# A hybrid block kernel: its compression weights in buffers of their own, and every weight remainder on VectorE

## The reference, cut to what matters

```python
proj = einsum('bsd,de->bse', rmsnorm(x), w_in[l])      # 1024 -> 3476 columns
# four heads of mLSTM, four of block attention, four of "native sparse attention" (NSA)
# NSA: two 64-wide streams kc, vc are compressed, blocks of 32 tokens at stride 16 -> 15 blocks
c = t.reshape(B, S // 16, 16, 64)
blocks = concatenate([c[:, r:15 + r] for r in range(2)], axis=2) + pe_
hid = silu(blocks.reshape(B, 15, 2048) @ w1_)          # w1_: 2048 x 128, one for kc, one for vc
return hid @ w2_
# the queries attend to the 15 compressed blocks (p_c), to selected blocks, to a window
x = x + mix @ w_out[l]
x = x + square(relu(rmsnorm(x) @ w_ff1[l])) @ w_ff2[l]
```

## Time and profile before

| | us |
|---|---|
| median of three runs | 1168.91 |
| lowest and highest of them | 1166.6, 1170.94 |
| the profiled execution, its own time | 1161.15 |
| its span in the trace | 1159.3 |
| granted TensorE clock, mean over the span | 0.984 |

### The profile page before, as it was taken

The page is one execution under the profiler, slowest core; times in us unless marked ns, Lnnn a source line. Parts: engine busy times, 40 slices in busy tenths (PEclk is TensorE's granted clock), DMA queues, the critical chain, the costliest instruction groups (busy, mean ns, idle before and its releaser), DMA issues.

```text
span 1159.3 us, 17421 instructions
## 1 busy us (share of the span) xinstructions
PE 1109.0 (96%) x6816; PEld 967.6 (83%) x6816; DVE 722.1 (62%) x1257; ACT 622.8 (54%) x981; POOL 115.5 (10%) x99
## 2 busy tenths in 40 slices
PE   8899989999999899989999999999999989999997
PEld 6787769899988787769899888798988767989885
DVE  4897667555556887667555656576355566744555
ACT  5545746544545445746444545465657446656562
POOL 0324110000000324110000000004000000040000
PEclk9999999999999998999999999999999989999999
DMA  8635235565666435236556565454443445544531
GB/s 300 192 94 179 86 116 183 184 194 184 182 184 186 142 93 177 87 117 199 181 186 187 178 197 183 157 170 145 128 145 110 145 146 164 154 137 120 154 127 55
DMA packets 88958, 181.15 MB, mean 156 GB/s; under 512 B 8669, under 2 KB 19805, under 8 KB 88877
## 3 DMA queue, kind: packets, MB, share of 16 engines
q1 hardware_dynamic: 87437, 175.78, 49.0%
q10 hardware_dynamic: 1440, 4.26, 1.0%
HBM read 178.97 MB, written 1.05 MB: 155 GB/s over the span
## 4 chain that ended last, share of the span: by engine, by line
PE 75%; DVE 13%; ACT 6%; issue 3%; POOL 1%; DMA 1%; DVEq 0%; POOLq 0%; SPq 0%; ACTq 0%
PE bank L757 22%; PE bank L759 21%; PE bank L758 21%; DVE w_lo L1572 2%; ACT w_hi L1207 2%; PE bank L834 2%; PE bank L872 1%; PE bank L919 1%; DVE vecs L1581 1%; DVE xn L1856 1%; PE bank L1015 1%; PE bank L1146 1%; DMA raw<-in_w_in 1%; PE bank L929 1%; PE bank L928 1%
## 5 line engine op out<-in xcount | busy, mean ns | idle before, releaser
L1572 DVE TENSOR_TENSOR w_lo<-raw,w_hi 128x1024 fp32r<-128x1024 f32 x296 | 365.3, 1238 | 312.3 <-ACT w_hi L1207 308.2
L1207 ACT ACTIVATE w_hi<-raw 128x1024 fp32r<-128x1024 f32 (+1 forms) x320 | 334.6, 1052 | 253.7 <-PE bank L759 222.6
L757 PE MATMUL bank<-h_hi,w_hi 128*128 128x256 f32 x896 | 259.9, 290 | 4.5 <-DVE w_lo L1572 2.1
L758 PE MATMUL bank<-h_lo,w_hi 128*128 128x256 f32 x896 | 255.2, 285 | 0.0
L759 PE MATMUL bank<-h_hi,w_lo 128*128 128x256 f32 x896 | 255.1, 285 | 0.0
L757 PE MATMUL bank<-w_hi,h_hi 128*128 128x512 f32 (+1 forms) x448 | 182.0, 406 | 5.8 <-DVE h_lo L1591 5.3
L757 PEld LDWEIGHTS bank<-h_hi,w_hi 128*128 128x128 f32 x896 | 173.6, 194 | 9.7 <-DVE w_lo L1572 3.1
L759 PE MATMUL bank<-w_hi,h_lo 128*128 128x512 f32 (+1 forms) x448 | 176.4, 394 | 0.0
L758 PE MATMUL bank<-w_lo,h_hi 128*128 128x512 f32 (+1 forms) x448 | 175.9, 393 | 0.0
L758 PEld LDWEIGHTS bank<-h_lo,w_hi 128*128 128x128 f32 x896 | 173.8, 194 | 0.5
L759 PEld LDWEIGHTS bank<-h_hi,w_lo 128*128 128x128 f32 x896 | 173.5, 194 | 0.0
(11 more groups left out here) (283 smaller groups left out, 1401.6 us busy)
## 6 DMA issues: line engine op xcount, KB each, us to landing
raw<-in_w_in SPq DMA_DIRECT2D x144, 512.0 KB, 3.9
raw<-in_w_ff SPq DMA_DIRECT2D x128, 512.0 KB, 4.1
raw<-in_w_out SPq DMA_DIRECT2D x40, 512.0 KB, 3.2
raw<-in_cmp_w SPq DMA_DIRECT2D x8, 512.0 KB, 4.5
raw<-in_w_in SPq DMA_DIRECT2D x8, 404.0 KB, 4.1
x_sb<-in_x SPq DMA_DIRECT2D x2, 512.0 KB, 7.4
gain<-in_norm_ffn ACTq DMA_DIRECT2D x2, 512.0 KB, 6.9
gain<-in_pre_norm ACTq DMA_DIRECT2D x2, 512.0 KB, 4.7
```

Source lines behind the costliest of these rows:

```text
L757: pe.matmul(out_ap, s_hi, m_hi, start=start, stop=False, **kw)
L758: pe.matmul(out_ap, s_hi, m_lo, start=False, stop=False, **kw)
L1207: act.activation(slot(w_hi, u), slot(raw, u), ACT.Copy).then_inc(hi_ready, 1)
L1572: dve.tensor_tensor(slot(w_lo, u), slot(raw, u), slot(w_hi, u).bitcast(F32), ALU.subtract)\
```

## The change

1. **Compression weights.** They leave the ring of `raw`. Four buffers that are idle at that time hold them: the two halves of `xn`, columns 1024 to 1535 of `mix`, and `gain`. SP loads each quarter (512 KB) with two transfers, behind the issue of units 5, 7, 9 and 11 of the layer (`load_cmp_weights`). Ahead of the first it waits until the last transpose of `xn` is done, ahead of the third (layer 0) until `sel` has been copied out of `mix`. The load of the next `gain` is issued by ScalarE after the compression products instead of after the norm.
2. **Compression products.** The blocks are stationary (32 columns), the weights move (128 columns); the sixteen chunks of each stream go in turn to four column groups of the array, at partitions 0, 32, 64 and 96 of one bank. ScalarE copies the four partial sums to `hid_parts`, and two short products with a 0/1 matrix (`C_SUM4`) add and transpose them (`hidden`).
3. **Turn 4** needs no doubled copy: eight products with the even or the odd columns of the identity put even tokens on partitions 0 to 63 and odd tokens on 64 to 127 (`even_odd_tokens`), and VectorE writes `blocksT` with two instructions instead of eight.
4. **Order.** Turn 4 goes from p 13 to p 12, `cmp` from p 16 to 18 to p 14 and 15, `hidden` to p 16, `cmp_kv` to 18, `cmp_kT` to 19, `cmp_s` and `cmp_soft` to 20, `cmp_o` from 25 to 26. The two `cmp_s` steps become one that alternates between them. The first `conv` waits for the compression products.
5. **`cmp_o`** is added straight to `mix` columns 768 to 1023.
6. **Remainders.** All 24 of GpSimd's go to VectorE.

```diff
-                proj_unit(0, l, w_in[l], j, bp, q, COLS1, "pool" if (p % 3 and p >= 13) or p in (9, 11) else "vector")
+                proj_unit(0, l, w_in[l], j, bp, q, COLS1, "vector")
...
-                if p == 11:
-                    step("vec_b", l, "copy")
                 if p == 12:
+                    single(0, "turn", l, 4)
                     single(4, "turn", l, 0)
...
+                if p == 14:
+                    use(("hidden_parts", l), 0)
+                    step("cmp", l, 0)
+                if p == 15:
+                    step("cmp", l, 1)
+                    done(("hidden_parts", l))
+                    step("hidden_parts", l)
                 if p == 16:
-                    use(("hidden", l), 2)
-                    cmp_unit(0, 0)
+                    single(3, "hidden", l)
...
+            def load_cmp_weights(n):
+
+                for l in range(L):
+                    at = n - unit_no["proj", 0, l, PROJ1[0], 0] - CMP_FIRST
+                    if at in (0, 2, 4, 6):
+                        k = at // 2
+                        if k == 0:
+                            filled(sp, ("norm", 2 * l, 1, 1))
+                        elif k == 2 and l == 0:
+                            sp.wait_ge(sel_ready, 1)
+                        w1 = cmp_w1[l, k // 2].rearrange("(h b a p) e -> h p b a e", p=P, a=4, b=2)[k % 2]
+                        for b in range(2):
+                            sp.dma_start(cmp_homes[k][:, b, :].rearrange("p (a e) -> p a e", e=P), w1[:, b]).then_inc(cmp_loaded[k], 16)
...
+            def even_odd_tokens(l, key):
+
+                for i in range(NT):
+                    drained(pe, ("proj", 0, l, 6, i))
+                ps = open_bank(key)
+                for v in range(2):
+                    for i in range(NT):
+                        for odd in range(2):
+                            mm = pe.matmul(ps[HD * odd:HD * odd + HD, v * P + HD * i:v * P + HD * i + HD],
+                                           rest[:, i, 1032 + HD * v:1032 + HD * v + HD], ident[:, odd:P:2], start=True, stop=True,
+                                           skip_group_check=True)
+                close(mm, key)
...
-                        for a in range(8):
-                            mm = pe.matmul(ps[:, 16 * v:16 * v + NC_CMP], w[:, a, :], blocksT[:, v, 8 * half + a, :],
-                                           start=(half == 0 and a == 0), stop=(half == 1 and a == 7))
-                        finish_unit(mm, s)
+                        for a in range(16):
+                            if a % 8 == 0:
+                                pe.wait_ge(cmp_loaded[2 * v + a // 8], 32 * (l + 1))
+                            g, at_col = 32 * (a % 4), NC_CMP * (16 * v + a)
+                            mm = pe.matmul(ps[g:g + 32, v * P:(v + 1) * P], blocks[:, at_col:at_col + 32], cmp_weights(v, a),
+                                           start=a < 4, stop=a >= 12, skip_group_check=True)
...
+                    elif kind == "hidden_parts":
+                        free(act.activation(hid_parts[:, :, :], src(s)[:, 0:T].rearrange("p (v e) -> p v e", v=2), ACT.Copy), s)
+                        load_gain(2 * l + 1)
...
-                        dst = mix[:, :, 1024:1280]
-                        free(dve.tensor_copy(dst, src(s)[:, :].rearrange("p (i c) -> p i c", i=NT)), s)
+                        dst = mix[:, :, 768:1024]
+                        free(dve.tensor_tensor(dst, dst, src(s)[:, :].rearrange("p (i c) -> p i c", i=NT), ALU.add), s)
```

More of the change, by code:

```diff
@@ L71 @@
 C_C01 = C_CNEG + NT * NC_CMP
[L72 removed]
+C_SUM4 = C_C01 + NT * NC_CMP
+C_END = C_SUM4 + 16
 def constants():
@@ L242, in m_values @@
             single(b, "mlstm", l, "O", h)
[L244 to L247, removed]
         for bp, j in enumerate(PROJ1):
@@ L598, in hybrid_blocks @@
         diag_ready = sem("diag_ready")
+        cmp_loaded = [sem(f"cmp_loaded{n}") for n in range(4)]
         half_neg_set = sem("half_neg_set")
@@ L1005, in _ @@
                     elif kind == "cmp":
[L1007 to L1010, removed]
+                        v = s[2]
+                        if v == 0:
+                            ps = open_bank(("hidden_parts", l))
                             pe.wait_ge(blocks_ready, l + 1)
-                        pe.wait_ge(raw_arrived[unit_no[s] % SLOTS], 16 * (unit_no[s] // SLOTS + 1))
-                        w = slot(raw, u)
-                        for a in range(8):
-                            mm = pe.matmul(ps[:, 16 * v:16 * v + NC_CMP], w[:, a, :], blocksT[:, v, 8 * half + a, :],
-                                           start=(half == 0 and a == 0), stop=(half == 1 and a == 7))
-                        finish_unit(mm, s)
+                        for a in range(16):
[4 more added lines that the diff above has]
+                                           start=a < 4, stop=a >= 12, skip_group_check=True)
+                        if v == 1:
+                            close(mm, ("hidden_parts", l))
+                    elif kind == "hidden":
+                        ps = open_bank(s)
+                        drained(pe, ("hidden_parts", l))
+                        for v in range(2):
+                            mm = pe.matmul(ps[:, 16 * v:16 * v + 16], hid_parts[:, v, :], const[:, C_SUM4:C_SUM4 + 16],
+                                           start=True, stop=True)
+                        close(mm, s)
                     elif kind == "cmp_kv":
@@ L1031, in _ @@
                     elif kind == "cmp_s":
-                        if s[2] == 0:
-                            drained(pe, ("turn", l, 5))
-                            drained(pe, ("cmp_kT", l))
-                        ps = open_bank(s)
-                        b = HD * s[2]
+                        if s[2]:
+                            continue
+                        drained(pe, ("turn", l, 5))
+                        drained(pe, ("cmp_kT", l))
+                        ps = [open_bank(("cmp_s", l, odd)) for odd in range(2)]
                         for i in range(NT):
```

98 lines of the change are left out of this document (46 added, 52 removed).

## The result

The changed kernel took 1138.42 us (median of four, 1137.7 to 1139.48), the kernel before, beside it, 1169.74 (1166.6 to 1170.94): ratio 0.9737, interval 0.9715 to 0.9759. Over all 73 executions of the kernel before that stood beside the experiments its median is 1167.9, from 1159.9 to 1173.6, and the mean granted clock falls from 0.987 in the shortest to 0.973 in the longest. The profiled one, 1161.15 us at 0.984, was one of the short ones; the median of the 73 is some 7 us longer.

A forecast was written before the change was run, and what follows sets the result against it. Up to 125 us TensorE's work and VectorE's lateness were taken to set the pace together. TensorE's 11.4 us per layer, capped by VectorE at 7.6, less 1.1, gave 6.5, 13 in all: 1168.91 - 13 = 1155.9 us, range 1147 to 1168.

The forecast's parts named there:

- The median of runs lies 7.8 above the profiled one, and I move it by the same: Last step, whole kernel: median stays 7.8 us above the profiled execution, so 1168.91 - 13 = 1155.9.
- VectorE allows less: Up to 125 us: VectorE's ledger (2.4) and its 5.22 us wait cap the gain at 7.6 us per layer.
- in-order waits: VectorE, being in order, also waits for `w_hi` where GpSimd did: 1.1 us per layer taken off, leaving 6.5.
- TensorE's ledger: TensorE's savings to 125 us: 2.4 + 3.8 + 0.1 + 1.8 + 1.7 + 1.6 = 11.4 us per layer.
- nearly free for VectorE: GpSimd's remainders moved to VectorE: 13.2 us added ahead of the last convolution, 13.0 of holding gone, net +0.2 per layer.
- Products: Compression products on TensorE, 64 instructions at 0.06 us in four column groups: 3.8 us instead of 7.56, -3.8 per layer.
- rival D: Column groups do not overlap: compression products cost 7.9 us instead of 3.8; -9 in all, 1160 us; chance 0.12.
- A: The forecast itself: -13 us, own range -7 to -19 (1150 to 1162); chance 0.48.
- Order of the chain: Compression chain two positions earlier: TensorE's waits shrink by 1.7 us for `kc_n`, 1.8 for `m_rows`, per layer.
- Clock: One of the two half-clock stretches up to 125 us goes: -1.6 us per layer.
- Rival E: Both half-clock stretches of each layer go and VectorE keeps up: 4 us more per layer, -21, 1148; chance 0.09.
- Rival C: VectorE's in-order queue waits at each of the 24 moved remainders: 25 us against 13, +12, 1181; chance 0.13.

The follow-up runs named there:

- e16: e7 with all four groups of 15-column compression products together at p 16 in bank 7: 18.6 us above e14.
- e12: e7 with 16 of the 32 float32 compression products per layer left out: 8.8 us less than e7.
- e8: The kernel before with own buffers for the compression weights, 24 remainders still on GpSimd: 1175.4 us, ratio 1.0076.
- e1: The kernel before with only GpSimd's 24 remainders moved to VectorE: ratio 0.9994.
- e7: The kernel before with own buffers for the compression weights and all remainders on VectorE: ratio 1.0013.
- e6: The changed kernel with the old form of the compression products (15 columns moving, no partial sums, bank 7): ratio 0.9841, 10.6 us above the changed kernel.
- e17: The changed kernel plus 32 unread float32 products per layer with 15 moving columns: 7.4 us from e18, 21.0 us lost to clock.
- e18: The changed kernel plus 32 unread float32 products per layer with 128 moving columns, one column group: 7.4 us from e17, 12.3 us lost to clock.
- e15: e14 with the 24 remainders back on GpSimd: 8.9 us above e14.
- e14: e13 with turn 4 as before: 11.2 us above the changed kernel.
- e10: The changed kernel with the four copies, four transposes and eight instructions of turn 4 as before: 1144.1 us.
- e3: The changed kernel with one column group instead of four and partial sums of 32 rows: ratio 0.977, 2 us above the changed kernel.
- e11: The changed kernel with 16 of the 32 float32 compression products per layer left out: no gain.
- e9: The changed kernel with the compression chain at its old places (products at p 16): 1145.3 us.
- e13: e9 with the partial sums in bank 7: equals e9's 1145.3 us.

## Why the prediction was wrong

The miss of 17.5 us has two parts of equal size.

**The median was moved by the same as the profiled execution (8.8 us).** "The median of runs lies 7.8 above the profiled one, and I move it by the same": this step failed. The profiled execution after took 1139.48 and the median is 1.1 below it. The kernel before has executions over 14 us apart, by their clock; so have e16 (11 us), e12 and e8 (7 each), with the same 15-column products. The kernels in the new form spread over 1 to 5 us. The offset went with the change, but the form of the products alone does not explain it: e1, e7 and e6 have the old form too and spread over 2.5 (ten executions), 4.5 (ten) and 0.7 us (four). That this form keeps the clock down is shown by e17 against e18; how the clock varies from execution to execution was only seen, and its cause stays open.

**The sum of the profiled execution (8.7 us).** 1148 was forecast for it. The mixing stages gave 19.7 us instead of 13, the feed-forward stages 2.5 instead of 0, the start and the rest took 0.6 back. The step that failed is "VectorE allows less": at most 7.6 us per layer, 6.5 with the in-order waits. To the start of `conv_silu`, counted from the squares, layer 0 went from 104.99 to 96.38 us and layer 1 from 105.70 to 93.81: 8.6 and 11.9. The windows of both layers (columns as in the earlier trace rows), before:

```profile
20.06:125.05 104.99, 96.88 (x626) 84.78 (x626) 84.13 (x211) 53.81 (x107) 34.62 (x25) 0.97 0.52 157
367.12:472.82 105.70, 97.96 (x624) 86.21 (x624) 82.01 (x206) 52.59 (x106) 35.00 (x25) 0.95 0.45 137
```

and after:

```profile
21.23:117.61 96.38, 88.46 (x642) 76.88 (x642) 80.64 (x213) 53.92 (x109) 5.76 (x13) 1.00 0.56 168
357.56:451.37 93.81, 87.92 (x632) 77.23 (x631) 79.66 (x207) 53.04 (x107) 5.92 (x13) 0.98 0.51 158
```

VectorE's busy time fell by 3.5 and 2.4 us, near the 2.4 of the ledger. Its idle time, what is left of each window, fell by 5.1 and 9.5, where the prediction allowed 5.22 at most and took 1.1 off. It had read that limit from one wait in layer 0; in layer 1 VectorE was idle for 23.7 us before and 14.2 after. TensorE's ledger said 11.4, close to layer 1, but its waits, of which 2.4 + 1.8 + 1.7 were to go, hardly went: TensorE's idle time in these windows went from 8.1 to 7.9 and from 7.7 to 5.9 us, as new waits (2.05 for `hid_parts`) took the place of old ones. What fell is its busy time, by 8.4 and 10.0: shorter products and time at 1.2 GHz.

Term by term:

- *Remainders, "nearly free for VectorE".* Right as a sum: over the whole trace VectorE's busy time in e1 against before is 723.0 against 722.1 with 24 remainders (24.3 us in their group) more, so 23.4 of holding went from its other work. Wrong as a price: undone in the changed kernel they cost 20.5 us, 15.4 at full clock and 5.1 of clock. A likely reason, argued and not shown: a held instruction in the chain of row maxima, `m_rows` and `kc_n` delays whatever waits behind it, while a remainder of the same length is made up to three units ahead. It pays only where the rest of the order is not late: 0 to 2 us in the order of before with the ring, 6.6 with own buffers (e7, e8), 8.9 in e15 against e14, 20.5 in the changed one.
- *Turn 4.* Forecast 2.6 us of VectorE per layer, measured 5.7 in all (e10), 3.9 of it at full clock: right in size.
- *Products.* 64 instructions took 2.16 us, not 3.8: rival D's mechanism fell, and the estimate between the ends should have been nearer the low one. But e3, which is rival D's case, is only some 2 us slower (4 were forecast between D and A), and e11 gains nothing. What the new form is worth, 10.6 us (e6), is 7.6 of clock, a term the forecast did not give to it.
- *Order of the chain.* It stands in the forecast as 1.7 us per layer for `kc_n` and a part of the 1.8 for `m_rows`, so up to 7 in all; measured 6.8 to 7.6 (e9, e13).
- *Clock.* One stretch per layer, 3.2 us in all, was counted. In the profiled executions 3.3 us went in all (5.1 in the mixing stages), so the size was near; over the means of all executions about 9 went, which belongs to the first part of the miss. The reading was wrong: the prediction set beside the first stretch that TensorE had been idle for 2.29 of 21 us up to 78, while in the 10 us just ahead of it, from 75.6 to 85.6, it was busy for 9.66 and ran 15-column products. Rival E's -21 is nearly what the profiled execution gained (21.7), yet not by its path: the two stretches of layer 0 up to 125 us went, and others came behind 125 us and ahead of the stage.
- *In-order waits.* 1.1 us per layer was charged; VectorE's only wait in 56 to 100 us is 0.65. To the start of `conv_silu` its waits for `w_hi` went from 3.7 to 6.6 us in layer 0, all ahead of that stretch, and from 4.8 to 3.7 in layer 1. Rival C's wait exists where the compression units go through the ring (7.84 us in e1).
- *Transfers.* No new wait of TensorE for weights: right.

The parts by undoing one at a time are 20.5, 10.6, 6.8 and 5.7, together 43.6 where the whole is 29.5: they overlap. A likely reason is that each alone makes VectorE or TensorE late for the other. The ladder e16, e14, e10 (or e13), after gives 18.6 + 5.5 (or 3.6) + 5.7 (or 7.6).

Open: why the feed-forward stages are 1.2 us shorter each (182.4 to 182.6 against 183.6 in every kernel built from the changed one, e14 and e15 too, and in none built from the one before; it lies in the products with `u_hi` and `u_lo`, whose mean is 391 to 393 ns against 394 to 396); why the clock varies so much more between executions of the kernel before; and why e12's clock did not rise. Not tried: moving more of VectorE's work between 57 and 100 us to ScalarE, which the full windows there suggest. No version that does all the work was faster than the changed kernel; one group, e3, has the highest clock, 0.992, and 2 us more.

## What to carry to other kernels

When two engines are both nearly full, don't cap a gain by the busy-time ledger of one and its longest wait in one layer: read its idle time in every layer, ask which single instructions on the chain between them are delayed, and price the parts together, since a part that gives 0 alone gave 20 us in the right order. Before forecasting a median from one profile, look at whether the spread goes with the granted clock, and don't take the offset over as it stands. Small products can be worth turning so that the long side moves, even if their own duration is the same; here that was worth 7.4 us for 64 extra instructions per layer.

## What the runs showed of the hardware

- Products with 128 stationary and 15 moving columns brought the granted clock down to 0.90 in a window where the same busy time of products with 128 moving columns left it at 1.00; TensorE hardly stood still in either (22.38 of 23 us busy). In e16 TensorE stayed near 1.2 GHz for most of 23 us (0.55) while busy for 21.44, behind a wait of 1.73 us. The Trainium skill (TensorE: Matmul & The Clock Gate, HAM oscillation — how this bites in real kernels) lays such a fall to waits between bursts of matmuls; e17 shows it without one, and the changed kernel's stretch at 125.1 us, behind 2.66 idle of 10 us, agrees with the Trainium skill.
- Four column groups overlap 3.4 times (2.16 against 7.36 us for 64 instructions with 128 moving float32 columns).
- 59.1 us more of GpSimd's elementwise work made VectorE's own 37.7 us longer and the kernel 40 us slower.
